# RWKV scan of a two-layer backbone: forward and backward chains share their hops, states kept undecayed

## What is computed

```python
def step(S, inp):
    w_t, k_t, v_t, a_t, b_t = inp[:5]
    sa = jnp.einsum('dbhij,dbhj->dbhi', S, a_t)
    S = S * w_t[..., None, :] + sa[..., :, None] * b_t[..., None, :] + v_t[..., :, None] * k_t[..., None, :]
    return S, jnp.einsum('dbhij,dbhj->dbhi', S, inp[5])
y = ys[0] + jnp.flip(ys[1], axis=1)            # forward + backward
yn = group_norm(y) * ln_w + ln_b
rk = jnp.sum((r[None] * k_dir).reshape(2, B, T, H, N) * r_k, axis=(0, -1))[..., None]
yn = yn + rk * v                               # the bonus
out = (yn * g) @ w_out
```

## Time and profile before

| | us |
|---|---|
| median of 3 runs | 2483.46 (2478.06 to 2487.39) |
| profiled execution | 2489.29, its span 2487.2 |
| PE busy | 2297.5 (92% of the span) |
| slot 1 (preparation, inversion) | 35.2 |
| slots 2 to 15 (all three) | 667.4 |
| slot 16 (inversion, chain) | 42.1 |
| slot 17 (chain, direct matmuls) | 33.0 |

### The profile page before, as it was taken

The page is one execution under the profiler, slowest core; times in us unless marked ns, Lnnn a source line. Parts: engine busy times, 40 slices in busy tenths (PEclk is TensorE's granted clock), DMA queues, the critical chain, the costliest instruction groups (busy, mean ns, idle before and its releaser), DMA issues.

```text
span 2487.2 us, 65185 instructions
## 1 busy us (share of the span) xinstructions
PE 2297.5 (92%) x27583; PEld 1901.2 (76%) x27583; DVE 1104.8 (44%) x2425; ACT 866.5 (35%) x1579; POOL 657.5 (26%) x481
## 2 busy tenths in 40 slices
PE   5998899899999999999988888888988889999998
PEld 3776677788888888878847777776776767888887
DVE  4236666351121112463366666666666645411213
ACT  3435555342121213352234334344244222422323
POOL 0334555212232332213311211111111110344442
PEclk8999999999999999999999999999999999999999
DMA  8125555112211221123410000000000011323321
GB/s 250 52 56 162 174 170 170 52 51 68 66 59 62 67 68 51 52 82 113 140 47 23 21 8 21 12 15 23 12 15 23 4 53 52 100 87 101 101 89 64
DMA packets 172316, 176.37 MB, mean 71 GB/s; under 512 B 26512, under 2 KB 160032, under 8 KB 172064
## 3 DMA queue, kind: packets, MB, share of 16 engines
q1 hardware_dynamic: 171200, 169.48, 21.8%
q10 hardware_dynamic: 864, 3.15, 0.3%
HBM read 161.06 MB, written 11.53 MB: 69 GB/s over the span
## 4 chain that ended last, share of the span: by engine, by line
PE 83%; DVE 7%; issue 5%; ACT 2%; SPq 1%; DMA 1%; POOL 1%; ACTq 0%; DVEq 0%
PE PS L397 38%; PE PS L1480 5%; PE PS L558 5%; PE PS L417 3%; PE PS L1465 2%; PE PS L756 2%; PE PS L737 2%; PE PS L1619 2%; PE PS L1455 2%; PE PS L1292 2%; PE PS L716 2%; PE PS L1564 1%; PE PS L746 1%; PE PS L1594 1%; PE PS L1123 1%
## 5 line engine op out<-in xcount | busy, mean ns | idle before, releaser
L377 POOL TENSOR_TENSOR WL<-RAW,WH 128x1024 fp32r<-128x1024 f32 x160 | 383.6, 2419 | 945.3 <-ACT WH L358 945.3
L397 PE MATMUL PS<-AH,WH 128*128 128x256 f32 (+1 forms) x992 | 350.8, 354 | 3.3 <-DVE AL L2358 2.4
L397 PE MATMUL PS<-AH,WL 128*128 128x256 f32 (+1 forms) x992 | 351.7, 355 | 0.0
L397 PE MATMUL PS<-AL,WH 128*128 128x256 f32 (+1 forms) x992 | 349.1, 352 | 0.0
L358 ACT ACTIVATE WH<-RAW 128x1024 fp32r<-128x1024 f32 x160 | 159.9, 1047 | 272.4 <-PE PS L397 265.7
L397 PE MATMUL PS<-BH,WL 128*128 128x512 f32 (+1 forms) x672 | 239.2, 356 | 0.0
L397 PE MATMUL PS<-BH,WH 128*128 128x512 f32 (+1 forms) x672 | 238.5, 355 | 0.0
L397 PE MATMUL PS<-BL,WH 128*128 128x512 f32 (+1 forms) x672 | 237.6, 354 | 0.0
L397 PEld LDWEIGHTS PS<-AH,WH 128*128 128x128 f32 x992 | 187.7, 189 | 31.6 <-issue 2.6
L397 PEld LDWEIGHTS PS<-AL,WH 128*128 128x128 f32 x992 | 187.0, 188 | 27.1
L397 PEld LDWEIGHTS PS<-AH,WL 128*128 128x128 f32 x992 | 187.4, 189 | 25.3
(11 more groups left out here) (270 smaller groups left out, 4874.6 us busy)
## 6 DMA issues: line engine op xcount, KB each, us to landing
ADW<-l_ada_w SPq DMA_DIRECT2D x40, 1024.0 KB, 5.3
RAW<-l_mlp_up SPq DMA_DIRECT2D x64, 512.0 KB, 4.5
RAW<-l_mlp_down SPq DMA_DIRECT2D x64, 512.0 KB, 4.0
RAW<-l_w_rkv SPq DMA_DIRECT2D x24, 512.0 KB, 5.2
rwkv_scratch<-STG SPq DMA_DIRECT2D x24, 384.0 KB, 3.4
ADA<-l_ada_w SPq DMA_DIRECT2D x4, 2048.0 KB, 12.1
RAW<-l_w_in SPq DMA_DIRECT2D x16, 256.0 KB, 5.4
RAW<-l_w_out SPq DMA_DIRECT2D x16, 256.0 KB, 5.3
```

The costliest lines, as they stand in the source:

```text
L377: e.tensor_tensor(WL[:, s, rows], RAW[:, s, rows], WH[:, s, rows], ALU.subtract).then_inc(w_split[h], 1)
L397: mm = e.matmul(dst, w[:, s, k, n * P:(n + 1) * P], r[:, k, lo:hi], start=(k == 0 and i == 0), stop=(k == KT - 1 and i == 2), skip_group_c ...
```

## The change

**Shared hops.** A hop now serves two passes. `runs(s, i)` lists what hop i of slot s carries: in an even slot (4 hops) the first four chunks of the forward pass s - 2 and the last four of the backward pass s - 3; in an odd slot (8 hops) chunks 4 to 11 of the forward pass s - 3 and the first eight of the backward pass s - 2. The two states lie side by side in SS, the right-hand sides in RH (128 x 2 x 64), and one DVE addition serves both. The forward delta is copied by DVE, the backward delta by ACT. There is one slot more (19), and the group norm of a group stands after the four hops of an even slot.

**States undecayed.** The decay SW is gone. SS keeps the state without its chunk's decay; the total of the chunk before is applied in the next update, where it is the scalar of one DVE instruction, and is multiplied into AR beforehand by POOL, in place (DECAYED, three or two instructions of together 1216 elements a partition), after the last matrix product of the preparation. POOL's first fill of XIT waits for that. The totals are copied to TOT, so WP needs two buffers.

**Bonus in preparation.** The product with r_k, its head sum on PE and the product with V move from the end of the chain to the odd slot's preparation; the results lie in X and OG until the group norm adds them. The transposes of V move later in the even slot's preparation.

**Storage.** AR, BKT and MT have four buffers; LV and the inverse are written into MT by ACT (LV in three instructions, not one), so LV and XIF are gone. G2G and RKS have one buffer; G2G is loaded in a queue entry of its own. ACT's split of the output projection's third block stands at the fifth hop of slot 17. SLOT has 90 and 97 letters, 41 of them c.

The diff, its core:

```diff
-            for s in range(NQ + 2):
+            for s in range(NQ + 3):
...
-                         "c": iter(chain(e, s - 2)) if s >= 2 else iter(())}
+                         "c": iter(chain(e, s)) if s >= 2 else iter(())}
...
+        DECAYED = (((1, 4, 1, 0), (4, 12, 2, 3)), ((0, 3, 1, 1), (4, 11, 2, 5), (11, 12, 2, 0)))
...
+            e.tensor_copy(totals(q), WP[w][:, :, at]).then_inc(ar_step, 1)
...
+            e.wait_ge(mat_done, 6 * q + 6)
+            e.wait_ge(ar_step, 2 * q + 1)
+            for lo, hi, wide, t0 in DECAYED[d]:
+                ins = e.tensor_tensor(AR[b][:, lo:hi, 0:wide, :].rearrange("p c a t -> p c (a t)"),
+                                      AR[b][:, lo:hi, 0:wide, :].rearrange("p c a t -> p c (a t)"),
+                                      totals(q)[:, t0:t0 + hi - lo].unsqueeze(2).to_broadcast([P, hi - lo, wide * C]), ALU.mult)
+            ins.then_inc(ar_step, 1)
...
+            e.wait_ge(ar_step, 2 * q + 2)
             e.wait_ge(rks_ready, q + 1)
             e.wait_ge(pads_ready, PADS)
...
+        def hops(s):
+
+            return 0 if s < 2 else 8 if s % 2 else 4
...
+            both = ((0, s - 3, 4 + i), (1, s - 2, i)) if s % 2 else ((0, s - 2, i), (1, s - 3, 8 + i))
+            return [(d, q, j, ORDER[d][j]) for d, q, j in both if 0 <= q < NQ]
...
+                    for d, q, j, c in now:
+                        side = (HALVES[1 - c % 2], HALVES[c % 2])
+                        for h, k in enumerate(HEADS):
+                            if j:
+                                mm = e.matmul(bank(5 + rh_at(s, d))[side[h], 0:HD], AR[q % 4][k, c, 0, :], SS[k, i % 2, d, :],
+                                              start=True, stop=True, skip_group_check=True)
                     mm.then_inc(rhs_done, 1)
...
+                delta_copy(e, lambda o, x: e.activation(o, x, ACT.Copy), s, i, 1)
...
-                        e.tensor_scalar(SW[:, :], SS[:, j % 2, :], total, None, ALU.mult).then_inc(sw_ready, 1)
...
+                delta_copy(e, e.tensor_copy, s, i, 0)
...
+                            ins = e.scalar_tensor_tensor(out=SS[:, 1 - i % 2, d, :], in0=SS[:, i % 2, d, :],
+                                                         scalar=totals(q)[:, before:before + 1], in1=new, op0=ALU.mult,
+                                                         op1=ALU.add)
...
+            def load_gate_weights(g):
+                sp.wait_ge(og_ready, g + 2)
+                sp.dma_start(G2G[:, :], a["l1_g2"][:, P * g:P * g + P]).then_inc(gate_loaded, 16)
```

426 lines of the change are left out of this document (244 added, 182 removed).

## The result

The changed kernel takes **2448.03 us** (median of 4 runs, 2446.91 to 2450.6) against 2482.27 (4 runs): 0.9867 of the kernel before, 95% interval 0.9846 to 0.9889. The gain is 34 us where 54 were forecast. The time lies in the forecast range.

A forecast was written before the change was run, and what follows sets the result against it. PE, busy 92% of the span, was taken as the bound. Slots 2 to 15 (-49), slot 16 (-9) and the tail (+4) sum to -54 us, 2429 us against the median of 2483.46; range 2395 to 2464.

The forecast's parts named there:

- the hops left over: Slots 2 to 15: 164 single chunks run instead of 168, at 0.62 us each, -3 us.
- Idle time ahead of chain steps: Slots 2 to 15: 84 hops fewer at 0.42 us of PE weight-load idle time each, -35 us.
- the sign named for it: Profile after: weight-load idle ahead of the chain lines near 30 us in slots 2 to 15, not 70.9.
- Shape changes: Slots 2 to 15: fewer switches between 128x64 and 64x64 matmuls on PE, some nops included, -5 us.
- Spacing: Slots 2 to 15: chain pieces stand wider apart and DVE loses work, so less remaining idle, -10 us (0 to -20).
- What is added: Slots 2 to 15: new ACT and POOL work, with a group-norm stall in even slots, +4 us (0 to +14).
- The check that was named: Prediction wrong if idle time ahead of the inversion's lines grows by what the chain's lines lose.
- The second rival: Slot length does not fall because the inversion's PE, DVE, ACT alternation sets it; only ends move, 2478 us; chance 0.08.
- Slot 16: Four double hops and a group norm replace 12 single hops: -9 us (-3 to -14), ending near 33 us.
- The tail: Slots 17 and 18: 20 chunks instead of 12 (+3), ACT's third-block split (+2), head sum gone (-1): +4 us.
- ACT and POOL taking a part back: Rival: late ACT copies and POOL's product blocking DVE cost 28 us in the slots, about 2457 us; chance 0.22.
- The slower one: Rival: POOL's scaling of AR delays XIT and the inversion; at 12 ns an element 2521 us; chance 0.08.

The follow-up runs named there:

- the best version: Changed kernel with V's first transposes early, slot 16's hops earlier, ScalarE's WI wait only in even slots, two of four table loads dropped: 2427.17 us, ratio 0.9771.

## Why the prediction was right, and where it was off

**The gain and its place.** Slots 2 to 15 gave 52.7 us for 49 forecast, and that the slots would be alike at about 44 us held (44.41 and 43.79). But the terms inside are not those of the sum, and that the totals agree is in good part luck: the forecast was a sum of idle time, and of PE's loads' idle time only 9.8 us went; 43.0 us are load time, for which it had only the -3 of the hops left over.

- *Idle time ahead of chain steps, -35 (-18 to -50).* It fell by 20 us, from 70.9 to 50.6, inside the bounds, near the low one; the sign named for it, 30 us, did not come. The term took a hop's price to be its idle time. It is more, because the steps' own latency is shared too: 84 hops fewer are 252 steps fewer. The weight loads of the chain lines fell by 39 us, and the second set of matmuls in the kernel before showed it directly, 0.22 us for a second direction in a hop of 0.97.
- By that price 84 hops fewer should save 84 x 0.75 = 63 us; 52.7 came. An estimate of where the 10 us went: an even slot would be 35.3 + 4 x 1.19 and the 1.5 us by which a slot with the group norm was longer before, 41.6 us, and an odd one 35.3 + 8 x 1.19 = 44.8. They are 44.4 and 43.8. The even slots keep back 2.8 us each, about 20 in all, and the odd ones give 7 more than this. That the even slots do not follow the chain's work is measured; the split is not.
- *Shape changes, -5.* The readings of the rows hold (0.2 us for a change and its return, on the spot), the step from there to the slot's length does not: 198 changes more cost 1.8 us, within scatter. The run adds changes to the changed kernel; that those taken from the kernel before were as free is argued.
- *Spacing, -10.* The part that came from DVE losing SW is 0 to 5 us (0.998 to 1.0002).
- *What is added, +4 (0 to +14).* At the upper end by the stalls themselves (29.4 us came, 14.6 went), and the place was only half seen. The group norm's stall went from the odd slots' end as said. The ones that came are ACT's too: 2.50 us behind the key rates in even slots and 1.69 us behind WI in odd ones. Of the second 1.3 us a slot were real, some 9 us in seven slots; it is a wait that odd slots do not need, in a place where the new order puts a chain step behind it. Of the first nothing is shown to be worth time: halved, it left the even slots at 44.1.
- *The check that was named: idle ahead of the inversion grows by what the chain's lines lose.* Its weight loads' idle time grew by 13 us (76.8 to 89.9) while the chain's lost 20. The second rival was thus partly true, in the even slots.

**Slots 0 and 1, not costed (0; +7.4).** 5.6 us are slot 0's. The step that failed is "the transposes of V move later in the even slot's preparation", which the front part tells and the prediction passed over. In pass 0 nothing runs beside the preparation, so the move is serial there, leaves PE idle 4.33 us earlier, and the clock goes to 1.2 GHz within that wait. Of slot 1's 1.8 us, the changed kernel run again had 0.6; what makes them is open.

**Slot 16, -9 (-3 to -14); -1.9.** The wrong step is "by latency: the inversion alone with four hops should end near 30". The runs with earlier hops and an earlier norm left it at 39 us, so it is not where the hops and the norm stand. PE has an idle time of 2.67 us at 1962.9 for which the profile names only issue; it was 2.91 before. The rest is open.

**The tail, +4 (+2 to +9); +5.2.** Held. In it are 1.5 us of a clock at 1.2 GHz behind PE's wait for the group norm, 7.6 in other executions, which no term had; and the 2.00 us of the wait itself lie in slot 16. (The sign "slots 17 and 18 near 37 together" is their twelve hops, 38.0 us.)

**The rivals.** ACT and POOL taking a part back: the time it gave (2457) was not reached, ACT's half is true with some 9 us, POOL's half is not, but for single slots (0 for a doubled product; in the best version one wait of 1.65 us behind it). The slower one fell: the product with an innermost broadcast took 2.08 us for 1024 elements, 2.0 ns an element where 9.5 were the break-even, and the row of L1510 names ACT and issue ahead of it, not POOL.

One slip in the texts ahead: the changed SLOT has 89 and 97 letters, 16 and 24 of them c, not 90 and 97 with 41, and the prediction's 41 of 187 pieces are 40 of 186. No term hangs on it.

## What to carry to other kernels

When two dependent chains are put side by side on TensorE, count a step's whole latency as shared, and price the second chain by what its matmuls add (here 0.22 us a hop beside 0.97), not by its idle time. Then look, slot by slot, for who is insensitive: doubling the chain's matmuls showed in one run that odd slots have no room for more chain work and even slots have. A price paid on the spot, like a change of shape, need not reach the total. A wait that every engine's string carries along, and that only one kind of slot needs, is cheap until a reordering puts the critical step behind it; and a 2 us wait of PE cost 1.5 or 7.6 us more through the clock, so a wait in front of long dense work is worth a look.
